# An SBUF layout in which streamed and held matmul operands no longer start at the same address modulo 2048

## The reference, cut to what matters

```
x = x + 1/2 * SwiGLU_1(RMSNorm(x))                      # D_FF = 2816
h = RMSNorm(x)
[xr | yr | q | k | v | g_a | g_b] = h @ w_in            # 1408, 1408, 3 x 1024, 2 x 1024
A = (GeLU(yr) * RG_LRU(conv4(xr))) @ w_up_a
B = chunked_attention(rms(q), rms(k), v, bias) @ w_up_b # 16 heads of 64
x = x + (sigmoid(g_a) * A + sigmoid(g_b) * B) @ w_out
x = x + 1/2 * SwiGLU_2(RMSNorm(x))
```

## Time and profile before

| | |
|---|---|
| median of 2 runs | 2781.64 us (2781.28 to 2782.0) |
| the profiled execution's own time | 2780.0 us |
| its span, first to last instruction | 2778.2 us |
| around the span | 1.8 us |
| granted TensorE clock, mean | 0.996 |
| PE busy | 2734.7 us, 98% |
| PEld busy | 2196.4 us, 79% |
| ACT, POOL, DVE busy | 1188.3, 1179.1, 833.2 us |

### The profile page before, as it was taken

One profiled execution on the slowest core, in us unless ns is written; L12 is line 12 of the kernel. 1 busy time (PEld: TensorE's weight loads), 2 busy tenths in 40 slices (PEclk: granted clock), 3 DMA queues, 4 the chain that ended last, 5 costly groups with the idle time before them and its releaser, 6 DMA issues.

```text
span 2778.2 us, 35532 instructions
## 1 busy us (share of the span) xinstructions
PE 2734.7 (98%) x11968; PEld 2196.4 (79%) x11968; DVE 833.2 (30%) x1515; ACT 1188.3 (43%) x1680; POOL 1179.1 (42%) x524
## 2 busy tenths in 40 slices
PE   7999999999999999999999999999999999999998
PEld 6888878878776688888888888788787757888887
DVE  4222035630015432221132211448100164322212
ACT  5443235742445534443243432457324364444422
POOL 3444444445442234444444444344453423444444
PEclk9999999999999999999999999999999999999999
DMA  7333223332331233332333323332333212333322
GB/s 259 99 91 102 94 85 97 91 100 84 98 98 41 71 91 99 98 98 91 100 99 98 92 91 99 87 93 84 110 96 97 72 40 88 95 91 99 98 92 91
DMA packets 247056, 263.82 MB, mean 95 GB/s; under 512 B 9040, under 2 KB 233072, under 8 KB 246928
## 3 DMA queue, kind: packets, MB, share of 16 engines
q1 hardware_dynamic: 242768, 253.70, 30.6%
q10 hardware_dynamic: 4160, 8.47, 0.9%
HBM read 259.95 MB, written 10.57 MB: 97 GB/s over the span
## 4 chain that ended last, share of the span: by engine, by line
issue 40%; PE 40%; POOL 18%; DVE 1%; POOLq 1%; ACT 0%; DMA 0%; DVEq 0%; ACTq 0%
POOL wlo L414 18%; PE ps L1095 10%; PE ps L1100 10%; PE ps L1099 10%; PE ps L1295 2%; PE ps L1223 2%; PE ps L1277 1%; PE ps L1208 1%; PE ps L1244 1%; PE ps L1239 1%; PE ps L1243 1%; POOLq L421 0%; POOLq L413 0%; PE ps L1325 0%; DVE p L1013 0%
## 5 line engine op out<-in xcount | busy, mean ns | idle before, releaser
L414 POOL TENSOR_TENSOR wlo<-raw,whi 128x1024 fp32r<-128x1024 f32 x475 | 1140.7, 2408 | 1464.1 <-ACT whi L463 1463.7
L1095 PE MATMUL ps<-h_lo,whi 128*128 128x512 f32 x2400 | 945.9, 394 | 21.8 <-DVE h_lo L748 9.8
L1100 PE MATMUL ps<-h_hi,wlo 128*128 128x512 f32 x2400 | 936.5, 390 | 0.0
L1099 PE MATMUL ps<-h_hi,whi 128*128 128x512 f32 x2400 | 936.4, 390 | 0.0
L463 ACT ACTIVATE whi<-raw 128x1024 fp32r<-128x1024 f32 x475 | 500.2, 1056 | 737.3 <-PE ps L1095 676.4
L1095 PEld LDWEIGHTS ps<-h_lo,whi 128*128 128x128 f32 x2400 | 452.0, 188 | 126.9 <-DVE h_lo L748 14.9
L1099 PEld LDWEIGHTS ps<-h_hi,whi 128*128 128x128 f32 x2400 | 452.4, 188 | 96.6 <-issue 3.8
L1100 PEld LDWEIGHTS ps<-h_hi,wlo 128*128 128x128 f32 x2400 | 452.0, 188 | 94.9
L1095 PE MATMUL ps<-act_lo,whi 128*128 128x512 f32 x704 | 273.9, 389 | 0.0
L1099 PE MATMUL ps<-act_hi,whi 128*128 128x512 f32 x704 | 273.9, 389 | 0.0
L1100 PE MATMUL ps<-act_hi,wlo 128*128 128x512 f32 x704 | 273.9, 389 | 0.0
(11 more groups left out here) (139 smaller groups left out, 2635.6 us busy)
## 6 DMA issues: line engine op xcount, KB each, us to landing
raw<-in_w_in SPq DMA_DIRECT2D x124, 512.0 KB, 3.7
raw<-in_w_gate SPq DMA_DIRECT2D x88, 512.0 KB, 3.7
raw<-in_w_up SPq DMA_DIRECT2D x88, 512.0 KB, 3.7
raw<-in_w_down SPq DMA_DIRECT2D x80, 512.0 KB, 3.4
raw<-in_w_up_b SPq DMA_DIRECT2D x19, 512.0 KB, 3.6
rel_band<-rel_rows ACTq DMA_DIRECT2D x1, 8192.0 KB, 39.7
raw<-in_w_out SPq DMA_DIRECT2D x16, 512.0 KB, 3.4
raw<-in_rg_band SPq DMA_DIRECT2D x14, 512.0 KB, 3.5
```

The costliest lines, as they stand in the source:

```text
L414: nc.gpsimd.tensor_tensor(wlo[:, s, :], raw[:, s, :], whi[:, s, :].bitcast(F32), ALU.subtract).then_inc(lo_made, 1)
L1095: ins = pe.matmul(ps[:, b, :], w_hi, x_lo, start=start, stop=False)
L1099: pe.matmul(ps[:, b, :], w_hi, x_hi, start=False, stop=False)
L1100: return pe.matmul(ps[:, b, :], w_lo, x_hi, start=False, stop=stop)
```

## The change

The tensors are put in another order with small gaps between some of them. `raw` comes right behind `x`, then `h_hi` and `whi`; 64 bytes are left free; then `wlo`; 64 bytes; `h_lo`; 128 bytes; `tmp`. All that lies in the reused region moves by 256 bytes, and `m_hi` and `m_lo` by a further 16 bytes, which rounding makes 32. Paddings at the end of two views shrink by 256 bytes, so that the region still fits and `v012` stays where it was modulo 2048. No instruction is added or removed, and none changes but in its addresses.

```diff
+APART = 64
...
         x = sb("x", [P, KD, S])
-        h_hi, h_lo = sb("h_hi", [P, KD, S], F32R), sb("h_lo", [P, KD, S], F32R)
         raw = sb("raw", [P, SLOTS, CW])
-        whi, wlo = sb("whi", [P, SLOTS, CW], F32R), sb("wlo", [P, SLOTS, CW], F32R)
+        h_hi, whi = sb("h_hi", [P, KD, S], F32R), sb("whi", [P, SLOTS, CW], F32R)
+        apart_64 = sb("apart_64", [P, 16])
+        wlo = sb("wlo", [P, SLOTS, CW], F32R)
+        apart_128 = sb("apart_128", [P, 16])
+        h_lo = sb("h_lo", [P, KD, S], F32R)
+        apart_256 = sb("apart_256", [P, 32])
         tmp = sb("tmp", [P, 2, S])
...
-                                        ("gate", [P, 2, S], F32), ("pad_f", [P, 2048 - 8], F32))
+                                        ("gate", [P, 2, S], F32), ("pad_f", [P, 2048 - 8 - APART], F32))
...
-            ("k", [P, KD, S], F32), ("p1", [P, TRI], F32), ("pad_g", [P, R - KD * S - TRI - 128], F32),
+            ("k", [P, KD, S], F32), ("p1", [P, TRI], F32), ("pad_g", [P, R - KD * S - TRI - 128 - APART], F32),
             ("v012", [P, 3, D], F32))
-        m_hi, _, m_lo = views(("m_hi", [P, KD, S], F32R), ("pad_h", [P, 3 * R - KD * S], F32),
+        _, m_hi, _, m_lo = views(("pad_m", [P, 4], F32), ("m_hi", [P, KD, S], F32R), ("pad_h", [P, 3 * R - KD * S], F32),
                               ("m_lo", [P, KD, S], F32R))
```

## The result

The changed kernel takes 2839.15 us (2838.67 to 2839.64, two runs) against 2781.64 us: slower by 57.5 us, ratio 1.0207, 95% interval 1.0163 to 1.0251. Its profiled span is 2836.9 us against 2778.2, at nearly the same granted clock (0.995 and 0.996). The predicted 2781.6 us and the range up to 2795 us were wrong.

A forecast was written before the change was run, and what follows sets the result against it. TensorE's 226.7 ns matmul step, 10,980 times, was taken to bound the kernel. 2780.0 us profiled plus 0 for changed and unchanged pairs, other engines and DMA, plus 1.6 against the median, gave 2781.6 us; range 2770 to 2795.

The forecast's parts named there:

- (1): Whole kernel: no instruction or wait is added, removed or reordered; only addresses change.
- (4): POOL, ACT and DVE access shifted addresses; slowdown stays hidden, on POOL if below a factor of two: taken as 0.
- (5): DMA into x_tok and tmp, 256 bytes off: taken as 0, with +5 us and +16 us as possible ends.
- part (3): Price of one matmul whose streamed and held operands' distance changes: taken as 0, for three reasons, over 8324 pairs.
- The load has room in its 226.7 ns: First reason for price 0: load is busy 188 ns, and 128 columns are in after some 0.11 us.
- Four held offsets and 48 steps gave one value: Second reason for price 0: held blocks at 0, 512, 1024 and 1536 bytes all give 226.7 ns steps.
- The matmul with no load beside it: Third, weightiest reason: before TensorE's pause at 855.3 us it records 388 ns, against 389 with a load, so no collision.
- Part (2): Which overlapping stream and load pairs move modulo 2048: 8324 matmuls changed, 2656 unchanged and put at 0.
- The bounds of part (3): Per changed pair: at best 11.5 ns gained, 96 us in all; at worst 13.3 ns lost.
- Faster: Rival: the 32-cycle surplus is a read collision; 2686 us if all goes, 2734 if half; chance 0.06 beyond 2%, 0.03 smaller.
- the mark that I named: Faster rival's sign: in products with h, two of three steps near 215 ns, h_hi beside next whi still 226.7.
- Slower: Rival: streams starting off a 512-byte boundary cost 32 cycles more; 5924 x 13.3 ns = 79 us, 2861 us; chance 0.04.

The follow-up runs named there:

- experiments 4 and 5: 4: TensorE alone, bursts of matmuls at many operand distances, no kernel time. 5: changed kernel, only the reused region, tmp and square moved by 256, or all gaps 256: 2780.27, 2780.19 us.
- experiment 8: TensorE alone: 15 aligned matmuls, then an odd one before a pause, with or without a pause ahead; odd held at 64 recorded 397 against 388 ns, or 502 each.
- Experiment 6: TensorE alone: finer distances, one odd matmul among seven aligned, product triples, fewer columns; aligned step 226.7 ns, one odd held at 64 costs 20 ns per eight.

## Why the prediction was wrong

The reading of what bounds the kernel held: TensorE's step is the time, and 65.1 us more of steps are 58.7 us more of span. So did parts (1), (4) and (5): POOL 2417 against 2408 ns, x_tok 5.0 against 4.9 us, tmp unchanged, and the runs of the order alone and of the region alone at the time before.

The step that failed is part (3), the price of one changed pair, taken as 0. Measured, it is 6.5 ns for an average matmul with h (233.3 against 226.8), 4.5 ns with act, ya and u, and 4.4 with m. Each of the three reasons failed in its own way.

- The load has room in its 226.7 ns: true (it is still recorded with 188 to 190 ns) and beside the point.
- Four held offsets and 48 steps gave one value: all the offsets were multiples of 512, hence of 256, the period that experiments 4 and 5 found. The rows were one point of the curve, sampled many times. I noted that no row showed another distance and still let them count as a reason.
- The matmul with no load beside it, called the weightiest: it was the wrong control. It was aligned itself, so it could show no cost of distance, and its own load had overlapped with the stream ahead, the one form in which experiment 8 finds the 9 ns; in the changed kernel the same record, with no load beside it, is 397 to 398 ns. From "a load beside the stream isn't what costs" I went on to "the layout can't cost".

Part (2) failed too, in a smaller way. "Unchanged pairs cost nothing" put 2656 matmuls at 0. Counted as there, by the load that runs beside the stream, the unchanged step with h is that behind h_hi with wlo: it went from 226.9 to 233.4 ns. Counted by a matmul's own operands it is h_hi with whi: from 226.8 to 235.7 ns, the most of the three. Experiment 6 shows a loss running on for three and more aligned matmuls.

The bounds of part (3) were -11.5 and +13.3 ns, and the truth lay inside. (By its own rows the first should be -11.7, half of 0.43 us being 215 ns; nothing hangs on that.) I closed the range at the middle on the strength of the third reason; with a price of 4 to 7 ns for all 10,980 matmuls the sum comes to 44 to 77 us, which holds the 57.5 measured. Unknown with both signs open, it asked for a range to about 2860 us.

The rivals. Faster: the mark that I named, two of three steps near 215 ns, isn't there. The surplus it lived on is 32 cycles for an aligned fp32r matmul of 512 columns as of 256, 320 and 384 (experiments 4 and 6), and no layout tried lowered it at 512; at 256 and 448 columns 64 bytes did lower it, by 2 to 3 ns. Slower: right sign, 79 us against 57.5, with a chance of 0.04. Its mechanism, a stream that starts off a 512-byte boundary, is not the one: all operands at 64 cost nothing (ratio 1.0003), streams at 256 cost nothing, and a held operand moved alone costs 43.0 us. That its price was near is luck: it doubled the surplus of 5924 steps and left the others alone, while nearly all steps grew, by 2 to 9 ns.

The Trainium skill, "SBUF — State Buffer", section "Who interferes with whom", gives TensorE two independent read ports and has PE wait on no one. For bf16 and plain float32 the runs agree: 215.8 and 429.2 ns at every distance tried. For fp32r they don't: 226.7 or up to 236.7 ns a step in a burst, by the distance alone, with no other engine at work. The 215.7 ns of "TensorE: Matmul & The Clock Gate", section "Wait — 56ns, not 53.3ns?", is met by bf16 (215.8) and missed by fp32r, by 11 ns at best.

What stays open is the mechanism: which two accesses meet, why the period is 256 bytes, why 64 costs 2 ns and 192 costs 7, why offsets of 4 and 16 bytes and fewer columns don't follow the same curve, and why one layout can fall into different rhythms. These runs give the shape of the loss at 512 columns, not its cause.

## What to carry to other kernels

For streams of fp32r matmuls of 512 columns, let all that TensorE reads, held and streamed, start at the same address modulo 256 bytes; more than that (2048) is not needed, and moving one tensor by 64 bytes costs 1.5% of this kernel. With fewer columns measure first: at 256 and 448 the aligned layout isn't the fastest. When rows agree over many samples, ask first in what they all agree: here, in being multiples of 512. And a control must be free of the suspect at the place where the loss would arise, not only at the place where it would be recorded.

## What the runs showed of the hardware that I had not expected

- An fp32r matmul of 512 columns steps in 226.7 ns (544 cycles at 2.4 GHz) when all starts agree modulo 256 bytes, and in 228 to 237 ns at nearly all other distances tried; a stream 4 bytes off took 236.7. The exceptions are a stream 252 bytes off, 226.7, and held at 16, 226.7 in one sweep and 233.2 in the other.
- An aligned fp32r matmul pays 32 cycles over its columns at 256, 320, 384 and 512 (120.0, 146.7, 173.4 and 226.7 ns), but 38 and 40 at 448 and 496 (202.7 and 223.3 ns). bf16 pays 6 cycles (215.8 ns for 512).
- With 256 columns a stream 64 bytes off is faster than the aligned one, 117.8 against 120.0 ns.
- Fewer held columns are no help: 230.0, 230.2 and 231.7 ns with 96, 64 and 32 of them, against 226.7 with 128.
- One matmul with its held operand 64 bytes off, among aligned ones, costs 20 ns in all: 9 on its own step, the rest on the three behind it. Held 128 off it costs 13, of which 6 fall on the step ahead; with the stream 64 off, 47 over eight steps.
